# Gathered rows of the second expert on partitions 96 to 127, and two gathers requested ahead of two broadcasts

## The reference

```python
def hier_moe(h, w_rg, b_rg, w_re, b_re, w_g, w_u, w_d):
    x = h.reshape(B * T, D)
    g_prob = jax.nn.softmax((x @ w_rg + b_rg), axis=-1)
    g_p, g_i = lax.top_k(g_prob, 1)                       # one of 4 groups
    e_logits = (x @ w_re + b_re).reshape(-1, MOE_GROUPS, MOE_PER_GROUP)
    e_sel = jnp.take_along_axis(e_logits, g_i[:, :, None], axis=1)[:, 0]
    e_v, e_i = lax.top_k(e_sel, MOE_TOPK)                 # two of its 8 experts
    gate = jax.nn.softmax(e_v, axis=-1) * g_p
    expert = g_i * MOE_PER_GROUP + e_i
    combine = jnp.sum(jax.nn.one_hot(expert, N_EXPERTS) * gate[..., None], axis=1)
    hid = jax.nn.silu(jnp.einsum('nd,edf->nef', x, w_g)) * jnp.einsum('nd,edf->nef', x, w_u)
    hid = hid * combine[:, :, None]
    y = hid.reshape(B * T, N_EXPERTS * D_EXPERT) @ w_d.reshape(N_EXPERTS * D_EXPERT, D)
```

## Time and profile before

| | us |
|---|---|
| median of three runs | 1083.04 |
| lowest, highest | 1081.32, 1086.36 |
| the profiled execution | 1080.98 |
| its span (first to last instruction) | 1079.1 |
| TensorE busy | 856.9 (79% of the span) |
| VectorE busy | 518.4 (48%) |
| ScalarE busy | 206.9 (19%) |
| GpSimd busy | 119.2 (11%) |

### The profile page before, as it was taken

One profiled execution on the slowest core, in us unless ns is written; L12 is line 12 of the kernel. 1 busy time (PEld: TensorE's weight loads), 2 busy tenths in 40 slices (PEclk: granted clock), 3 DMA queues, 4 the chain that ended last, 5 costly groups with the idle time before them and its releaser, 6 DMA issues.

```text
span 1079.1 us, 17024 instructions
## 1 busy us (share of the span) xinstructions
PE 856.9 (79%) x6432; PEld 463.0 (43%) x6432; DVE 518.4 (48%) x1235; ACT 206.9 (19%) x428; POOL 119.2 (11%) x196
## 2 busy tenths in 40 slices
PE   3799999998769995675678997899499995756840
PEld 0355455554435552342333465446255562323420
DVE  1257523345546773423454465534657664324353
ACT  2222332122111210100122115211022120101111
POOL 2300012200401110000000000110211110000000
PEclk9899999998879997878898999999699997878885
DMA  9982442938989999999998523011799999999911
GB/s 308 367 303 78 156 156 91 381 118 339 344 309 340 394 381 391 397 405 398 417 385 330 175 81 125 28 56 59 293 378 396 388 378 395 406 397 399 417 75 58
DMA packets 75123, 304.61 MB, mean 282 GB/s; under 512 B 8440, under 2 KB 8752, under 8 KB 49576
## 3 DMA queue, kind: packets, MB, share of 16 engines
q1 hardware_dynamic: 66072, 277.08, 67.2%
q0 software_dynamic: 7696, 21.77, 6.1%
q10 hardware_dynamic: 1280, 4.72, 1.1%
HBM read 304.51 MB, written 5.32 MB: 287 GB/s over the span
## 4 chain that ended last, share of the span: by engine, by line
PE 61%; DMA 25%; DVE 5%; SPq 3%; ACT 3%; issue 2%; POOL 0%; ACTq 0%; DVEq 0%; POOLq 0%
DMA ring<-in_w_exp_up 19%; PE psum L721 16%; PE psum L1055 13%; PE psum L1020 5%; PE psum L1077 4%; PE psum L793 4%; PE psum L919 4%; PE psum L745 3%; SPq L442 2%; PE psum L1009 2%; DMA ring<-in_w_in_odd 2%; DMA ring<-in_w_mod 2%; DMA arena<-h_rows,arena 2%; PE psum L967 1%; PE psum L1186 1%
## 5 line engine op out<-in xcount | busy, mean ns | idle before, releaser
L1055 PE MATMUL psum<-ring,arena 128*32 128x256 f32 x2816 | 200.9, 449 | 101.7 <-issue 58.3
L1055 PEld LDWEIGHTS psum<-ring,arena 128*32 128x32 f32 x2816 | 106.7, 129 | 208.7 <-issue 123.1
L1869 DVE TENSOR_TENSOR ht<-ht,psum 128x512 f32<-128x512 f32 x276 | 172.8, 680 | 41.8 <-PE psum L1020 41.6
L721 PE MATMUL psum<-ring,ht 128*128 128x512 f32 (+1 forms) x432 | 170.3, 552 | 3.4 <-ACT ht L1254 2.7
L1896 DVE TENSOR_TENSOR arena<-arena,psum 64x256 f32<-64x256 f32 x44 | 18.2, 413 | 217.4 <-ACT arena L1400 217.4
L721 PEld LDWEIGHTS psum<-ring,ht 128*128 128x128 f32 x432 | 81.5, 191 | 85.7 <-issue 77.1
L1020 PE MATMUL psum<-y_top,to_token 64*128 64x512 f32 x276 | 94.7, 459 | 4.1 <-DVE y_low L1905 4.0
L1077 PE MATMUL psum<-ring,arena 128*32 128x512 f32 x704 | 85.5, 604 | 0.0
L1020 PE MATMUL psum<-y_low,to_token 64*128 64x512 f32 x276 | 85.4, 414 | 0.0
L745 PE MATMUL psum<-ring,cond_silu 128*32 128x512 f32 x384 | 49.1, 647 | 26.0 <-DMA ring<-in_w_mod 26.0
L1400 ACT ACTIVATE arena<-psum 64x256 f32<-64x256 f32 x44 | 16.7, 380 | 265.5 <-PE psum L1055 265.5
(11 more groups left out here) (318 smaller groups left out, 892.9 us busy)
## 6 DMA issues: line engine op xcount, KB each, us to landing
ring<-in_w_exp_gate SPq DMA_DIRECT2D x32, 2048.0 KB, 18.6
ring<-in_w_exp_up SPq DMA_DIRECT2D x32, 2048.0 KB, 23.7
ring<-in_w_exp_down SPq DMA_DIRECT2D x32, 2048.0 KB, 24.9
ring<-in_w_mod SPq DMA_DIRECT2D x24, 2048.0 KB, 19.0
ring<-in_w_in_even SPq DMA_DIRECT2D x5, 2048.0 KB, 19.9
shift_scale<-mod_rows POOLq DMA_DIRECT2D x3, 2048.0 KB, 11.1
ring<-in_w_in_odd SPq DMA_DIRECT2D x3, 2048.0 KB, 19.7
ring<-in_w_out_even SPq DMA_DIRECT2D x2, 2048.0 KB, 8.4
```

The lines of the kernel that those rows point to most:

```text
L721: mm = pe.matmul(psum[:, to, 0:cols], HT[:, b, k, :], w[:, k, :], start=(k == 0), stop=(k == KC - 1))
L1055: mm = pe.matmul(psum[to:to + SLOTS, 2, 0:256], XT[:, k, SLOTS * e:SLOTS * (e + 1)], RG[:, 3 * u + a, e, k, :], start=(k == 0), stop=(k == ...
L1869: dve.tensor_tensor(acc, acc, bank(BACK_BANKS[c]), ALU.add).then_inc(M("added"), 1)
```

## The change

`XS[v]` gets all 128 partitions. The first expert's rows stay on partitions 0 to 31, the second's go to 96 to 127. The gather takes its row numbers from all 128 partitions; the products of the first table are computed for both halves of the partitions (as those of the big table were), and a new constant column `unused` puts the row numbers of partitions 32 to 95 out of bounds. Turning the rows is now an ordinary matrix product with 128 partitions of rows as the stationary operand and 64 columns of the identity (0 to 31 and 96 to 127) as the moving one, so that `XT` is as before. On GpSimd gathers 2 and 3 stand ahead of the two broadcasts. On TensorE the sum of "places" stands ahead of the wait for the big table's operands. The values computed are the same.

```diff
-        XS = [vx(D, parts=2 * SLOTS) for _ in range(2)]
+        XS = [vx(D) for _ in range(2)]
...
+                                  np.where((i // SLOTS) % 3 == 0, 0.0, NOWHERE).astype(np.float32)[:, None]], axis=1),
...
                 def gather(q, v, static=False):
-                    row = one(first_row[0:2 * SLOTS, q:q + 1]) if static else column(0, q)
-                    pool.tensor_copy(one(from_row[v][0:2 * SLOTS, 0:1].bitcast(U32)), row).then_inc(M("row_looked_up"), 1)
+                    row = one(first_row[:, q:q + 1]) if static else column(q)
+                    pool.tensor_copy(one(from_row[v][:, 0:1].bitcast(U32)), row).then_inc(M("row_looked_up"), 1)
                     pool.wait_ge(M("row_looked_up"), q + 1)
                     pool.sem_inc(S("pool_waited"), 1)
-                    pool.indirect_dma_start(XS[v], None, h_rows[l], bass.IndirectOffsetOnAxis(ap=from_row[v][0:2 * SLOTS, 0:1].bitcast(U32), axis=0),
+                    pool.indirect_dma_start(XS[v], None, h_rows[l], bass.IndirectOffsetOnAxis(ap=from_row[v][:, 0:1].bitcast(U32), axis=0),
...
                 if l == 0:
                     store_rest("places")
+                for v in range(2):
+                    one_pass(v, v, static=True)
                 load_rows(u, (2, 3), gt_t[:, :], "gate_in")
                 if l == 0:
                     load_rows(2, (0, 2), gs_t[:, :], "rows_in")
-                for v in range(2):
-                    one_pass(v, v, static=True)
...
                 for i in range(6):
-                    mm = pe.matmul(psum[0:2 * SLOTS, 5, 0:4], in_slot[:, i, :], in_first[:, i, :], start=(i == 0), stop=(i == 5))
+                    for side in range(2):
+                        rows = slice(2 * SLOTS * side, 2 * SLOTS * (side + 1))
+                        mm = pe.matmul(psum[rows, 5, 0:4], in_slot[:, i, :], in_first[:, i, :], start=(i == 0), stop=(i == 5))
                 mm.then_inc(S("routing_ps"), 1)
+                if l == 0:
+                    mod_sum(mods("places")[0])
                 pe.wait_ge(S("routing_sb"), 3 * l + 3)
...
                 mm.then_inc(S("routing_ps"), 1)
-                if l == 0:
-                    mod_sum(mods("places")[0])
+                both_sides = ident[:, :].rearrange("p (a s) -> p a s", a=4)[:, 0:4:3, :]
...
                     for k in range(KC):
-                        t = pe.transpose(psum[:, 0, 2 * SLOTS * k:2 * SLOTS * (k + 1)], XS[v][:, k:D:KC], ident[0:2 * SLOTS, 0:2 * SLOTS])
+                        t = pe.matmul(psum[:, 0, 2 * SLOTS * k:2 * SLOTS * (k + 1)], XS[v][:, k:D:KC], both_sides, start=True, stop=True)
...
-                dve.tensor_tensor(tab[:, 0, :], tab[:, 1, :], tab_tmp, ALU.add).then_inc(S("table_ready"), 1)
+                dve.tensor_tensor(tab[:, 0, :], tab[:, 1, :], tab_tmp, ALU.add)
+                dve.scalar_tensor_tensor(tab[:, 1, :], tab[:, 1, :], unused, tab_tmp, ALU.max, ALU.add).then_inc(S("table_ready"), 1)
```

More of the change, by code:

```diff
@@ L93, in shape_constants @@
         "k_rope": rope,
-        "k_dest": np.broadcast_to(1.0 + i[:, None, None] + (T * np.arange(2))[None, :, None] + (P * np.arange(NB))[None, None, :],
-                                  (P, 2, NB)).astype(np.float32).reshape(P, 2 * NB).copy(),
+        "k_dest": np.concatenate([np.broadcast_to(1.0 + i[:, None, None] + (T * np.arange(2))[None, :, None] + (P * np.arange(NB))[None, None, :],
+                                                  (P, 2, NB)).astype(np.float32).reshape(P, 2 * NB),
+                                  np.where((i // SLOTS) % 3 == 0, 0.0, NOWHERE).astype(np.float32)[:, None]], axis=1),
     }
@@ L270, in build @@
         q_ms, q_rs, q_rt = ([sm(12), sm(12), sm(6)] for _ in range(3))
-        dest = sm(6)
+        dest_unused = sm(7)
+        dest, unused = dest_unused[:, 0:6], dest_unused[:, 6:7]
         cond_silu = cond_t[:, :].rearrange("p (k m) -> p k m", m=34)
@@ L534, in _ @@
             load(iota[:, :], d["k_iota"], "state_in")
-            load(dest, d["k_dest"], "state_in")
+            load(dest_unused, d["k_dest"], "state_in")
             pool.memset(S0.rearrange("p a h v -> p (a h v)"), 0.0).then_inc(S("pool_steps"), 1)
@@ L606, in experts, with column @@
                     store_rest("router")
-                def column(field, q):
-                    return tab[0:2 * SLOTS, field:field + 1, bass.ds(q, 1)]
+                def column(q):
+                    return tab[:, 1:2, bass.ds(q, 1)]
                 def one(v):
@@ L1830, in experts @@
                 dve.wait_ge(S("routing_ps"), 4 * l + 3)
[L1831 to L1836, removed]
+                found = psum[:, 5, 0:4]
+                link(dve.tensor_scalar(first_tmp, found, 0.0, NOWHERE, ALU.is_equal, ALU.mult))
+                link(dve.scalar_tensor_tensor(first_row, found, -1.0, first_tmp, ALU.add, ALU.add))
+                link(dve.tensor_scalar(first_tmp, first_row, float(T), float(-T), ALU.is_ge, ALU.mult))
+                dve.scalar_tensor_tensor(first_row, first_row, unused, first_tmp, ALU.max, ALU.add).then_inc(S("table_ready"), 1)
                 link(dve.tensor_tensor(in_pair[:, :, 0, :], across(PLACES), along(slot_c, PLACES), ALU.is_equal))
```

## The result

The changed kernel takes 1136.95 us (median of four runs, 1136.12 to 1140.50) against 1082.18 us of the kernel before on the same chips: ratio 1.051 (95% interval 1.047 to 1.056), **slower by 55 us**. The forecast was 1070, the range 1058 to 1090. The profiled execution has a span of 1134.3 us; the sum on record stands for a span of 1065.8 (1067.7 less the 1.9 around it), so the profile has 68.5 us to explain.

What follows compares the result with a forecast made beforehand. Each expert layer's first part was taken as TensorE-bound, its second as DMA-bound. Layer 0 -13.7, layer 1 -0.6, tail +1.0 gave -13.3 us: 1067.7 profiled, 1069.7 against the median, forecast 1070, range 1058 to 1090.

Steps and rivals of the forecast that it cites:

- the sum on record: Whole kernel: layer 0 -13.7, layer 1 -0.6, tail +1.0, together -13.3 us, giving 1067.7 for the profiled execution.
- part 2: Turning rows on TensorE (L1009): block 2.0 us instead of 1.07, +1.0 us a pass, nothing for the strided read.
- The rival on strided loads: L1009, first part's passes: strided loads cost more in two-load form; 1097 at 60 ns a load, 1121 if doubled; chance 0.15.
- Part 1: Order of GpSimd's requests: pass 2's wait for its gather goes, gaining 13.8 us in layer 0, none in layer 1.
- Part 3: Where rows land, second part of each layer: spread rows slow the DMA less, 0.6 us gained a gather.
- the gather's 1.1 us: Second part of each layer: a pass takes 16.10 us, weights alone 15.0 at 420 GB/s, so a gather costs 1.1.
- No relief: DMA in the second part: gathered rows slow it wherever they go, passes of 16.1 and 16.2, about 1080; chance 0.17.
- The stall in part: Pass 2 of layer 0: its rows take 14 us to land, 4 us of TensorE wait remain, 1075; chance 0.08.
- the +1.0 of the tail: Tail of layer 1: one more turning block lies there and adds 1.0 us.
- 60 ns a load: Turning loads at L1009: upper bound for the stride's cost, 1.0 us a pass more.

Runs made afterwards that it cites:

- the contiguous run: The changed kernel with its turning products (L1014) reading eight contiguous blocks of 128 channels instead of every eighth channel: 1080.1 us, ratio 0.999.
- the cheaper turning: The changed kernel with each block turned by seven single-load transposes over all 128 partitions and one ordinary product for the last 64 columns: 1063.6 us, ratio 0.983.

## Why the prediction was wrong

**The step that failed** is the stride in part 2: "I take nothing", because strided transposes follow one another about as closely as contiguous ordinary loads, "as if each form had one limit of this size and the two didn't add". They do add, and by more than the upper bound of that sum: a strided load in the two-load form starts every 0.237 us, a contiguous one every 0.112. That is 2.0 us a pass, where the bounds were nothing and 1.0. I had the row that spoke against it (200 against 140 ns) and explained it away with the distance between starts. That distance was no evidence: in the transposes the stride lengthens each load from 140 to 200 ns, but the time from one start to the next hardly shows it (0.110 us; L710's contiguous ones 0.109). The rival on strided loads named this mechanism, its place (L1009) and even the doubled size (1.9 us a pass; measured 2.03, the 11.43 less 9.40). It gave 1121 for it, 51 us on top of the forecast; the runs have 1127.6 without the clock's share, 47.5 us on top of the contiguous run. Its chance of 0.15 was too low, and the range left out most of it.

**What no case held**: the clock. I took TensorE's clock for given in every case. Behind strided blocks of 64 moving columns it fell to 0.50, behind contiguous ones and behind strided ones of 128 columns it didn't: 9.3 us of the whole. Without this share the time would still be 1127.6 us.

**The other steps**, by the profile. Part 1: right in the stall (gone), optimistic in the start. Turning pass 0's rows began at 284.22 instead of 280.15 in this execution. The delay is there already at the first table's products, which began at 266.22 before:

```profile
270.40 0.87 PE L997 MATMUL psum<-arena 128*64 128x4 f32 x24
```

Over the thirteen profiles of the study these begin between 266.2 and 271.8 us, with and without the change, and the turning between 280.0 and 285.1, so I take it for scatter that one execution can't average. And gate/up of pass 0 took 5.52 us, at a granted clock of 0.65. The 2.0 us of a contiguous block and the 9.36 us of its pass were right (2.00 and 9.40). Part 3 was right in its direction, and its size, 15.47 against 15.5, by luck: I took half of the gather's 1.1 us because full slots still lie side by side, but the drop in the rate is gone altogether. What the gather still costs is about its own bytes: an estimate from the rows is 6.29 MB of weights and some 39 rows of 4 KB at 419 GB/s, 15.4 us. "No relief" falls. The stall in part falls as well (landing after 8.2 us, needed 8.2 us later still).

The sums by place: pass 21 of layer 0 began at 564.78, forecast 526.1, 38.7 late: 6.0 at the gate/up of pass 0 (289.12 for 283.1; 4.2 of late start, 2 of the longer block), 7.1 more up to pass 2 (314.97 for 301.8: two long passes, both in part at a lowered clock), 26.0 over the ten passes to pass 12 (11.96 less 9.36), -0.4 from there to pass 21 (1.8 more up to pass 14, 2.2 less behind it). Layer 1 adds 29.8 (1084.01 against the 1015.5 of the sum); from there to the end are 50.3 us against 49.2 before, the +1.0 of the tail. 38.7 and 29.8 are the 68.5.

**One more term was too small** in all cases: pass 12 to pass 14. I allowed 1.5 us in which nothing moves after pass 11's products, and 0.5 for each gather, and got 22.1 us. With contiguous loads it was 25.2 us in both layers: 3.1 us twice. Two windows of that run, in layer 0:

```profile
396.00:398.00 2.00, 2.00 (x32) 1.33 (x24) 0.34 (x2) 0.38 (x1) 0.00 (x0) 1.00 0.36 133
398.00:400.00 2.00, 2.00 (x19) 1.80 (x19) 0.37 (x2) 0.59 (x1) 0.19 (x1) 1.00 0.68 143
```

The DMA moved only 133 and 143 GB/s over these four microseconds, and then the weights that the next passes waited for had to pass at 420. This, the start of pass 0 (4.2 us) and its lowered clock (2.9) come to 13.3 us; smaller differences the other way leave the 12.6 by which the contiguous run's span (1078.4) exceeds 1065.8. (Its layer 1 routes other data, as its layer 0 computes something else.)

## To carry to other kernels

When a transpose becomes an ordinary fp32 product, its stationary operand is loaded twice, and a stride that the one form hides shows in full in the other: price a form and a stride together, from a row that has both (the bound put together from their single prices, 60 ns a load, was half of what it cost). With fp32 data a stride of two elements cost next to nothing here, one of four or eight doubled such a load; a wide transpose that computes columns nobody needs can be cheaper than an exact product (8.87 us a pass against 11.96). And where a gather competes with a stream of weights, spread its rows over both halves of the partitions: that was worth 0.5 to 0.7 us of each 16 us pass here, and with the order of requests and the cheaper turning 1.7% in all (1063.6 us).

## What the hardware showed beside this

**The clock fell in step with the loop.** The same code alternated between full and lowered clock from pass to pass in layer 0 and fell in every pass in layer 1 (stride of four); with 128 moving columns in place of 64, and loads of equal length, it stayed at 1.00 throughout the first part from pass 2 on.

**Rows out of bounds are read.** The page's queue and memory lines, of the kernel before and of the changed one:

```profile
q0 software_dynamic: 7696, 21.77, 6.1%
...
HBM read 304.51 MB, written 5.32 MB: 287 GB/s over the span
```

```profile
q0 software_dynamic: 10768, 21.78, 5.6%
...
HBM read 317.10 MB, written 5.32 MB: 284 GB/s over the span
```

Each of the 48 gathers lists 64 more rows, all out of bounds: 3072 more packets, and the memory reads 12.6 MB more, 4 KB for each, while the bytes moved stay the same. In the passes that the DMA bounds no cost of it can be seen (15.47 us a pass, 0.6 less than before). A run with the rows spread and fewer rows listed wasn't made.
